# Eighteen weight-chunk casts per mixer on ScalarE instead of VectorE, with the mixer's order laid anew

## The chip, the cores and the metric

One core of one Trainium2 chip runs the whole forward pass. The metric is the device time of one execution in microseconds (us), the median of several. A core has TensorE (PE, matmuls; PEld is its weight loading), VectorE (DVE), ScalarE (ACT), GpSimd (POOL) and SyncE (SP, which here only issues DMAs). Each engine takes its own instruction stream in order. They meet only at semaphores.

## The reference

Two layers over 528 tokens (16 meta tokens and 512 real ones) of width 1024, batch 1. Each layer is a mixer and a convolutional feed-forward network, with fp32 inputs and outputs:

```
xn   = rms_norm(h, norm1_g);  proj = xn @ w_in        # 1024 -> 5288
fq, fk, fv, ff, cq, ckv, krope, sq, sk, sv, gates = split(proj)
out_a = causal_attention(norm(fq), norm(fk), fv, cumsum(log_sigmoid(ff + b)))   # 8 heads x 64
q     = norm(norm(cq) @ w_q_up);  k, v = norm(ckv) @ w_kv_up (+ krope), rope    # 8 heads x 96
out_b = causal_attention(q, k, v)
out_c = sliding_window_attention(norm(sq), norm(sk), sv, sinks, alibi)          # 8 heads, 2 kv heads
h     = h + sum_n(sigmoid(gates_n) * (out_n @ w_branch_n)) @ w_o
u     = rms_norm(h, norm2_g) @ w_up                    # 1024 -> 5632
h     = h + (silu(gate) * val) @ w_down                # gate, val = causal conv of width 3 over u
```

## The kernel before, in words

Weights come from HBM as blocks of 128x128. Eight blocks make a chunk (128x1024 fp32, 512 KB), and 135 chunks make a layer: 61 for the mixer up to the last branch product, then w_o, w_up and w_down. To keep fp32 accuracy each operand is split into a rounded high part and a low part that holds the rest. A block is then three products (high by high, high by low, low by high: L1357, L1360, L1362), each over the two halves of the 528 tokens, so six matmuls.

A chunk passes four stations:

- SP loads it into one of two raw buffers (`load`, L734). It waits until the low part of the chunk two before is made, since that frees the buffer.
- DVE casts it to its high part `wh` (`high_part`, L1670), one of three buffers. It waits for the load and until TensorE has started the chunk two before the cast one.
- POOL subtracts to make the low part `wl` in four pieces (`chunk_low`, L817), after the cast.
- TensorE waits at the first block of a chunk for that (`weights`).

Cast and low part of chunk c stand in their engines' streams where TensorE's stream has block 8(c - 2) of the layer (AHEAD is 2).

The mixer is one list of steps for all engines. `mixer_plan` lays the tiles of the projections in a given ORDER. A tile is 128 output rows: `fq0` is the first pair of query heads of the fox attention, `gF0` a gate tile, `yF0` a product with w_branch, and it takes 8 blocks (y 4, mq 2, mk and mv 1). Every other step gets a block index. The step "newton" of a normed tile stands 4 blocks after its end plus a LATE value, or at BEGIN[job - 2] + 13 if that is later. "norm" is one further on and "high" (ACT's copies of the normed tile into its operands, POOL's low part) two. Twelve attention jobs, each of a pair of heads (4 fox, 4 sliding-window, 4 latent), begin at the indices in BEGIN:

- From BEGIN - 25 the job's scores for the row maximum are computed ("M", L1501) and reduced on DVE (L1962, last the meta rows "MM" at L1940).
- At BEGIN - 4 "NT" transposes the maxima (L1509), and ACT copies them into the query's extra row.
- At BEGIN the scores proper ("STM", "ST", L1540 to L1546) are masked by DVE (L1972, L1985), exponentiated by ACT (L1255, L1258, L1272, L1274) and multiplied with the values ("PV", L1588) two indices later.
- After the second head come four reciprocals on DVE (L1993), the product with them (L1998), and the split of the heads into high and low part.

Each engine's stream is this list sorted by index, with a shift by LAG for chosen pairs of engine and step. So the order is fixed by hand on every engine, and a late instruction holds back all behind it on its engine. START gives the indices, counted from the end of the first tile, of the decay rows of the fox attention ("decay", "decay2"), their way through SP ("extras", L764 and L771) and POOL ("extras2", L918), and the rope rows (L1915 to L1927). ZERO_FIRST and ZERO_AT place POOL's fills of constant rows (L831).

The statistic of an mq tile (L1376) waits for DVE's two products (L1830, L1832), which empty its slot of PSUM.

Of the kernel before, what the change touches and what calls it, by code (L numbers as in the profile page):

```python
# [33 lines left out]
BLK = 8  # L34
CW = BLK * P
RAW, SPLIT = 2, 3
AHEAD = 2
OT_RING = 6
G_RING = 4
PT_RING = 3  # L40
ZERO_FIRST = [0 + n * 2 for n in range(10)]
ZERO_STEP = 2

OFF = np.cumsum([0, 512, 512, 512, 8, 256, 128, 32, 512, 128, 128])
# [36 lines left out]
STAT_LAG = 2  # L81
NORM_LAG = 4
RS_LEAD = 17
BEGIN = [65, 94, 122, 161, 192, 222, 250, 282, 319, 354, 384, 429]
ORDER = 'fk0 gF0 fv0 fq1 fk1 gF1 fk2 fq2 fv1 fk3 fv2 fq3 gF2 sq0 sk gF3 fv3 gF4 sq1 sq2 sv gF6 gF5 yF0 gF7 cq0 cq1 yF1 sq3 yF2 yF3 ckv yF4 yF6 mq0 yF5 mv0 mq1 yF7 gS0 mk0 gS2 mv1 mq2 gS1 gS3 mq3 yS0 mk1 yS1 mq4 gS4 mv2 mq5 yS2 gS5 mk2 gS6 mq6 yS3 gS7 mq7 yS4 yS7 yS5 mk3 gM0 mv3 gM6 gM4 yS6 gM1 gM5 gM7 gM2 gM3'
M_LEAD = 25
M_STEP = 1.8
NT_LEAD = 4
# [1 line left out]
PV_LAG = 2  # L90
ST_END = 13
ZEROS = 10
ZERO_AT = 17
FIRST_STAT = 1
FIRST_LEAD = 16
FIRST_STEP = 0.8
START = [12, 16, 4, 18, 21, 26, 11]
LAG = {('dve', 'layer stat'): 1, ('dve', 'M'): 1, ('dve', 'MM'): 1, ('act', 'O'): -1, ('pool', 'high'): 2, ('act', 'head copy'): 1, ('act', 'tanh'): -1, ('dve', 'rope2'): 1, ('dve', 'decay'): 1, ('dve', 'rope'): 2, ('act', 'inverse'): 4, ('dve', 'heads'): 2, ('act', 'VT'): -1, ('dve', 'join'): 1, ('dve', 'VT'): 1, ('pe', 'MM'): 1, ('dve', 'turn'): 1}

LATE = {'sk': 2, 'cq': 2, 'fv': 1}


def constants():
# [48 lines left out]
    return out  # L154


class Signal:


# [15 lines left out]
class Tile:  # L175


    def __init__(self, kind, m, i):
        self.kind, self.m, self.i = kind, m, i
        self.nk = BLOCKS[kind]  # L180
        self.slot = i % 2
        self.freed = None
        self.joint = None
        self.n = None
        self.raw = None


def mixer_plan():
# [27 lines left out]
    for s in range(2):  # L216
        mine = [t for t in tiles if t.slot == s]
# [4 lines left out]
    events = []  # L222
# [71 lines left out]
    for j, (br, p) in enumerate(JOBS):  # L294
# [17 lines left out]
        for e in range(2):  # L312
            for t in range(5):
                i = b + ST_HEAD * e + t
# [4 lines left out]
        i = b + ST_HEAD + 4 + PV_LAG + 2  # L319
        for q in range(4):  # L320
            put(i + q, 6, "recip", j, q)
        if j >= OT_RING:
            i = max(i, end_of["y", (JOBS[j - OT_RING][0], KD - 1)] - 3)
# [3 lines left out]

    plan = {"tiles": tiles, "order": order}
    for engine in ("pe", "dve", "act", "pool", "sp"):
        mine = [(i + LAG.get((engine, step[0]), 0), rank, n, step) for i, rank, n, step in events]  # L330
        mine = sorted(blocks + mine, key=lambda x: x[0:3])
        plan[engine] = [x[3] for x in mine]


    turn, holder = 0, [None, None, None]
    for s in plan["pe"]:
# [27 lines left out]
        turn = (turn + 1) % 3  # L364
# [21 lines left out]
PLAN = weight_plan(mixer_plan()["order"])  # L386
CHUNKS = DEPTH * len(PLAN) // BLK
# [3 lines left out]
def build(nc, W, H, PRM, CST, POS, OUT, SCR, counts):  # L391
    plan = mixer_plan()
    tiles, order = plan["tiles"], plan["order"]
    LB = len(PLAN)
# [12 lines left out]
    raw = sb("raw", [P, RAW, CW])  # L407
    wh = [sb(f"wh{i}", [P, CW], F32R) for i in range(SPLIT)]
# [44 lines left out]
    sq = sb("sq", [P, 2, T])  # L453
# [48 lines left out]
        return ps[slot][:, CENTRE + j * TH:CENTRE + (j + 1) * TH]  # L502

    signals = []

    def S(name):
        s = Signal(nc, name, counts)
# [7 lines left out]
    s_out = nc.alloc_semaphore("output_stored")  # L515
    s_raw = [nc.alloc_semaphore(f"chunk_loaded{i}") for i in range(RAW)]
    s_hi = nc.alloc_semaphore("chunk_high_part")
    s_lo = nc.alloc_semaphore("chunk_split")
    s_start = nc.alloc_semaphore("chunk_started")
    ready_made = S("small_tiles_ready")  # L520
# [6 lines left out]
    copied = S("tile_copied")  # L527
    squared = S("tile_squared")
# [78 lines left out]
    def frees(t):  # L607
        if t.kind == "ff":
            return rope_copied, ()
        if t.kind in NORMED:  # L610
            if t.kind == "cq" and t.m == 0:
                return copied, (t.i,)
            return (stat_copied if t.kind == "mq" else stat_taken), (t.i,)
        if t.kind in ("fv", "sv"):
            return values_scaled, (t.kind, t.m)
        if t.kind == "mv":
            return values_copied, (t.kind, t.m)
        if t.kind == "g":
            return gate_taken, t.m
        return gate_used, t.m  # L620
# [102 lines left out]
    block = nc.Block()  # L723
    with block as blk:
# [75 lines left out]
        def _(pool):  # L800
# [9 lines left out]
            def chunk_low(c):  # L810
                if c >= CHUNKS:
                    return
                pool.wait_ge(s_hi, c + 1)
                settled()
                for a in range(0, CW, CW // 4):
                    part = slice(a, a + CW // 4)
                    ins = nc.gpsimd.tensor_tensor(wl[c % SPLIT][:, part], raw[:, c % RAW, part],  # L817
                                                  wh[c % SPLIT][:, part].bitcast(F32), ALU.subtract)
                ins.then_inc(s_lo, 1)
                began["last"] = (s_lo, c + 1)  # L820
# [33 lines left out]
            for l in range(DEPTH):  # L854
                n_blocks = 0
                for s in plan["pool"]:
# [9 lines left out]
                    elif s[0] == "zero":  # L866
                        i, n = s[1], s[2]
# [39 lines left out]
                    elif s[0] == "extras2":  # L907
                        j = s[1]
                        br, p = JOBS[j]
                        i = j % 2  # L910
# [3 lines left out]
                        c0, n = (1, T) if br == FOX else (0, TK)  # L914
# [19 lines left out]
                    elif s[0] == "high":  # L934
                        t = s[1]
                        if t.kind in ("fq", "sq"):
                            j = FIRST_JOB[SWA if t.kind == "sq" else FOX] + t.m
                            i = j % 2
# [8 lines left out]
                        elif t.kind == "fk":  # L947
                            j = t.m
                            i = j % 2
# [58 lines left out]
        def _(act):  # L1008
# [39 lines left out]
            for k in range(KD):  # L1048
                if k % 2 == 0:
                    act.wait_ge(s_hin[k // 2], 16)  # L1050
                high_input(0, k)
                nc.scalar.activation(merged[:, k, :], h[:, k, :], ACT.Square).then_inc(
                    residual_squared.sem, residual_squared.tick((-1, "dn", k)))
            for l in range(DEPTH):
                for s in plan["act"]:
                    if s[0] == "layer stat":
                        if s[1] != (l == 0):
                            continue
                        logarithms()
# [2 lines left out]
                    elif s[0] == "done":  # L1062
                        t = s[1]
# [21 lines left out]
                        elif t.kind == "mv":  # L1085
                            act.wait_ge(tile_ready.sem, tile_ready.at(l, t.i))
                            n = value_sets.index(f"{t.kind}{t.m}")
# [4 lines left out]
                    elif s[0] == "stat":  # L1092
                        t = s[1]
                        n = MEAN_OF[t.kind]
# [37 lines left out]
                    elif s[0] == "high":  # L1132
                        t = s[1]
# [10 lines left out]
                        if t.kind in ("fq", "sq", "fk"):  # L1144
                            act.wait_ge(raw_taken.sem, raw_taken.at(l, t.i))
                            dst, high, a = (xk, key_high, 1) if t.kind == "fk" else (xq, query_high, 0)
# [33 lines left out]
                    elif s[0] == "kfill":  # L1180
                        j, e = s[1], s[2]
                        i, kv = j % 2, JOBS[j][1] // 2
# [24 lines left out]
                    elif s[0] in ("VT", "VE"):  # L1207
                        t, second, place = s[1], s[2], s[3]
                        n = value_sets.index(f"{t.kind}{t.m}") + second
# [11 lines left out]
                        for e in range(2):  # L1221
                            c = second if window else e
# [20 lines left out]
                    elif s[0] == "STM":  # L1243
# [8 lines left out]
                        if br == SWA:  # L1252
                            for e in range(2):
                                c = PC_SB + 2 * p + e
# [5 lines left out]
                    elif s[0] == "ST":  # L1260
                        _, j, e, t, place = s
                        br, p = JOBS[j]
                        k0, nk, q0, nq = key_tile(br, t)
                        i = pt_slot(j, e, t)
# [5 lines left out]
                        if br == SWA and t == 0:  # L1270
                            c = PC_SB + 2 * p + e
# [46 lines left out]
                for f in range(FT):  # L1318
                    for side, dst in ((0, cg), (1, cv)):
                        t = 2 * f + side  # L1320
# [341 lines left out]
        def _(dve):  # L1662

            def high_part(c):
                if c >= CHUNKS:
                    return
                dve.wait_ge(s_raw[c % RAW], 16 * (c // RAW + 1))
                if c >= SPLIT:
                    dve.wait_ge(s_start, c - SPLIT + 2)
                nc.vector.tensor_copy(wh[c % SPLIT][:, :], raw[:, c % RAW, :]).then_inc(s_hi, 1)  # L1670

            def advance(l, i):
                n = l * LB + i
                if n % BLK == 0 and n > 0:
                    high_part(n // BLK + AHEAD)
# [91 lines left out]
            for l in range(DEPTH):  # L1767
                n_blocks = 0
# [412 lines left out]
```

## Time and profile before

| what | us |
|---|---|
| median of 3 runs | 1979.04 |
| lowest, highest | 1978.89, 1981.82 |
| profiled execution, first to last instruction (its span, the only time it has) | 1979.4 |
| PE busy | 1914.7 (97%) |
| DVE, POOL, ACT busy | 1159.0 (59%), 1025.5 (52%), 766.2 (39%) |

The two mixers take 31 to 556 us and 1011 to 1540 us of the span. The rest is feed-forward, apart from the first 31 us. The profile's page divides the span into 40 slices of 49.5 us. TensorE is busy for 9 tenths or more in all but three: the first two, and the one at 1039 us, where the second layer has just begun. Engines that are not TensorE are never full. In such a kernel the gaps of TensorE are to be read one by one, with what ended each.

### The profile page before, as it was taken

How to read it: one execution, taken by the hardware profiler on the slowest of the kernel's cores; microseconds unless marked ns; L12 is line 12 of the kernel's file. 1: busy time of each engine (PE TensorE's matmuls, PEld its weight loads, DVE VectorE, ACT ScalarE, POOL GpSimd, SP SyncE). 2: the span in 40 equal slices, each digit the busy share in tenths (PEclk: the TensorE clock that was granted, in tenths of full speed). 3: DMA queues.
4: the chain of work that ended last, by engine and by line, in shares of the span. 5: the costliest groups of instructions: out<-in, count | busy, mean ns of one | idle time of the engine just before them, and what ended most of it. 6: DMA issues, size and time to landing. Idle time of an engine off the chain costs nothing.

```text
span 1979.4 us, 36478 instructions
## 1 busy us (share of the span) xinstructions
PE 1914.7 (97%) x14396; PEld 1817.1 (92%) x14396; DVE 1159.0 (59%) x2121; ACT 766.2 (39%) x1514; POOL 1025.5 (52%) x1306
## 2 busy tenths in 40 slices
PE   7899999999999999999998999999999999999999
PEld 7889998888999999999997899988889999999887
DVE  7665476787465666552256654767874655665411
ACT  5455666655223222220044556666553232222100
POOL 7655454544364444544477455544443645445553
PEclk9999999999999999999999999999999999999999
DMA  4212121211232322332332121112112423323332
GB/s 149 75 44 65 54 65 44 63 45 55 65 129 85 97 86 86 97 93 93 93 109 76 43 65 54 63 46 65 45 53 65 141 86 97 97 86 96 96 97 96
DMA packets 44802, 156.30 MB, mean 79 GB/s; under 512 B 5012, under 2 KB 5268, under 8 KB 44504
## 3 DMA queue, kind: packets, MB, share of 16 engines
q1 hardware_dynamic: 44488, 153.75, 24.7%
q8 instruction: 114, 1.87, 0.4%
q14 instruction: 56, 0.46, 0.1%
q10 hardware_dynamic: 144, 0.22, 0.0%
HBM read 149.63 MB, written 4.26 MB: 78 GB/s over the span
## 4 chain that ended last, share of the span: by engine, by line
PE 77%; DVE 12%; ACT 4%; issue 3%; POOL 2%; DMA 1%; SPq 0%; DVEq 0%; ACTq 0%; POOLq 0%
PE ps L1357 20%; PE ps L1360 19%; PE ps L1362 19%; PE ps L1588 5%; PE ps L1372 2%; PE ps L1368 2%; PE ps L1371 2%; PE ps L1376 2%; DVE osum L1993 1%; DVE rstd L1691 1%; PE ps L1540 1%; PE ps L1501 1%; POOL wl L817 1%; DVE ps L1962 1%; DVE square L1686 1%
## 5 line engine op out<-in xcount | busy, mean ns | idle before, releaser
L817 POOL TENSOR_TENSOR wl<-raw,wh 128x256 fp32r<-128x256 f32 x1076 | 798.7, 773 | 746.5 <-DVE wh L1670 739.9
L1357 PE MATMUL ps<-xh,wh 128*128 128x264 f32 (+1 forms) x2880 | 810.7, 303 | 12.5 <-DVE wl L1750 9.4
L1360 PE MATMUL ps<-xl,wh 128*128 128x264 f32 (+1 forms) x2880 | 764.3, 286 | 0.0
L1362 PE MATMUL ps<-xh,wl 128*128 128x264 f32 (+1 forms) x2880 | 585.4, 285 | 0.0
L1357 PEld LDWEIGHTS ps<-xh,wh 128*128 128x128 f32 x2880 | 546.7, 190 | 31.1 <-issue 18.3
L1360 PEld LDWEIGHTS ps<-xl,wh 128*128 128x128 f32 x2880 | 547.4, 190 | 17.0 <-issue 8.9
L1362 PEld LDWEIGHTS ps<-xh,wl 128*128 128x128 f32 x2880 | 451.2, 190 | 0.0
L1670 DVE CAST wh<-raw 128x1024 fp32r<-128x1024 f32 x270 | 206.6, 765 | 176.0 <-PE ps L1357 89.1
L1588 PE MATMUL ps<-pt,vx 128*128 128x512 f32 (+7 forms) x480 | 157.8, 409 | 3.9 <-ACT pt L1274 2.3
L1985 DVE TENSOR_TENSOR ps<-ps,cst 128x128 f32<-128x128 f32 (+6 forms) x240 | 74.8, 313 | 145.3 <-PE ps L1546 111.0
L1274 ACT ACTIVATE pt<-ps 128x256 f32<-128x256 f32 (+5 forms) x224 | 78.5, 363 | 112.5 <-DVE ps L1985 111.2
L1324 ACT ACTIVATE cv<-ps,prm 128x528 f32<-128x528 f32 (+1 forms) x44 | 34.6, 786 | 209.0 <-DVE ps L2039 209.0
L1357 PE MATMUL ps<-oth,wh 128*128 128x264 f32 (+1 forms) x384 | 111.5, 312 | 2.1 <-ACT ssum L1011 1.7
L2039 DVE TENSOR_TENSOR ps<-ps,rstd 128x528 f32<-128x528 f32 (+1 forms) x88 | 62.1, 706 | 80.5 <-PE ps L1362 80.4
L1360 PE MATMUL ps<-otl,wh 128*128 128x264 f32 (+1 forms) x384 | 100.9, 283 | 0.0
L1993 DVE RECIPROCAL osum<-osum 128x132 f32<-128x132 f32 x96 | 90.0, 958 | 13.2 <-ACT oraw L1011 13.0
L1360 PE MATMUL ps<-al,wh 128*128 128x264 f32 x352 | 93.1, 285 | 0.0
L1357 PE MATMUL ps<-ah,wh 128*128 128x264 f32 x352 | 93.0, 284 | 0.0
L1540 PE MATMUL ps<-xq,xk 97*17 97x16 f32 (+15 forms) x288 | 78.2, 290 | 8.8 <-ACT ptm L1255 4.0
L1501 PE MATMUL ps<-xk,xq 96*128 96x400 f32 (+13 forms) x256 | 71.6, 300 | 9.1 <-DVE nm L1962 3.0
L1588 PEld LDWEIGHTS ps<-pt,vx 128*128 128x128 f32 x480 | 74.6, 191 | 6.2 <-ACT pt L1274 4.1
L1001 POOL TENSOR_TENSOR otl<-oraw,oth 128x528 fp32r<-128x528 f32 x24 | 34.5, 1437 | 87.5 <-ACT oth L1011 86.7
(194 smaller groups left out, 3440.9 us busy)
## 6 DMA issues: line engine op xcount, KB each, us to landing
raw<-weights SPq DMA_DIRECT2D x270, 512.0 KB, 3.5
h<-tokens SPq DMA_DIRECT2D x4, 528.0 KB, 6.9
h<-tokens SPq DMA_DIRECT2D x8, 264.0 KB, 6.0
residual<-h SPq DMA_DIRECT2D x8, 264.0 KB, 5.0
h<-residual SPq DMA_DIRECT2D x8, 264.0 KB, 5.9
out<-h SPq DMA_DIRECT2D x8, 256.0 KB, 4.7
cst<-constants SPq DMA_DIRECT2D x1, 1048.0 KB
extra<-positions SPq DMA_DIRECT2D x18, 4.1 KB
```

The source lines that it names most:

```text
L817: ins = nc.gpsimd.tensor_tensor(wl[c % SPLIT][:, part], raw[:, c % RAW, part], wh[c % SPLIT][:, part].bitcast(F32), ALU.subtract)
L1274: ins = nc.scalar.activation(pt[0:nk, i, 0:nq], bank[0:nk, 0:nq], ACT.Exp)
L1357: a = nc.tensor.matmul(out, a_hi, x_hi[:, sl], start=first, stop=False)
L1360: nc.tensor.matmul(out, a_hi, x_lo[:, sl], start=False, stop=False)
L1362: ins = nc.tensor.matmul(out, a_lo, x_hi[:, sl], start=False, stop=last)
L1501: ins = nc.tensor.matmul(bank[:, col:col + nk], xq[rows, i, e, q], xk[rows, i, e, k0:k0 + nk], start=True, stop=True)
L1540: nc.tensor.matmul(out, xk[rows, i, e, keys], xq[rows, i, e, q], start=True, stop=False)
L1588: ins = nc.tensor.matmul(heads_out[:, c:c + nq], vals, pt[:, i, 0:nq], start=t == 0, stop=t == 4)
L1670: nc.vector.tensor_copy(wh[c % SPLIT][:, :], raw[:, c % RAW, :]).then_inc(s_hi, 1)
L1985: nc.vector.tensor_tensor(sc, sc, cst[0:nk, a:a + n], ALU.add).then_inc(scores_masked.sem, scores_masked.tick((l, j, e, t)))
L1993: nc.vector.reciprocal(osum[:, a:a + T // 4], osum[:, a:a + T // 4]).then_inc(dve_step.sem, dve_step.tick((l, "recip", j, q)))
L2039: nc.vector.tensor_tensor(src[:, skip:T], src[:, skip:T], rstd[:, skip:T], ALU.mult).then_inc(up_scaled.sem, up_scaled.tick((l, t)))
```

## The change

Three things change.

- In each layer the casts of 18 chunks (of the 61 that are made while the mixer runs) move to ACT as `activation(Copy)`. They have a semaphore of their own, `s_hi_act`, on which POOL waits for these chunks. ACT takes such a cast at the block index where DVE had it, with the same two waits.
- The order of tiles, the beginnings of the jobs, START, LATE, LAG, ZERO_FIRST, ZERO_AT and FIRST_STEP get other values, and one single step (`turn mq4` on DVE) is placed one index later (FINE).
- The slot of the tile cq0 is free for TensorE once ACT has squared it, where before it was free once ACT had copied it.

```diff
-ZERO_FIRST = [0 + n * 2 for n in range(10)]
+ZERO_FIRST = [-1, -1, 0, 5, 6, 8, 10, 12, 12, 21]
-BEGIN = [65, 94, 122, 161, 192, 222, 250, 282, 319, 354, 384, 429]
-ORDER = 'fk0 gF0 fv0 fq1 fk1 gF1 fk2 fq2 fv1 fk3 fv2 fq3 gF2 sq0 sk gF3 fv3 gF4 sq1 sq2 sv gF6 gF5 yF0 gF7 cq0 cq1 yF1 sq3 yF2 yF3 ckv yF4 yF6 mq0 yF5 mv0 mq1 yF7 gS0 mk0 gS2 mv1 mq2 gS1 gS3 mq3 yS0 mk1 yS1 mq4 gS4 mv2 mq5 yS2 gS5 mk2 gS6 mq6 yS3 gS7 mq7 yS4 yS7 yS5 mk3 gM0 mv3 gM6 gM4 yS6 gM1 gM5 gM7 gM2 gM3'
+BEGIN = [65, 93, 122, 161, 191, 222, 250, 282, 319, 354, 386, 422]
+ORDER = 'gF0 fk0 fv0 fq1 fk1 gF1 fq2 fv1 fk2 fk3 fv2 fq3 gF2 sq0 sk gF3 fv3 gF4 sq1 sq2 sv gF6 gF5 yF0 cq0 cq1 sq3 yF2 gF7 yF1 yF3 ckv yF4 yF6 mq0 yF5 mv0 mq1 yF7 gS0 mk0 gS2 mv1 mq2 gS1 gS3 mq3 yS0 mk1 yS1 mq4 gS4 mv2 mq5 yS2 gS5 mk2 gS6 mq6 yS3 gS7 yS5 mq7 yS7 yS4 mk3 gM0 mv3 yS6 gM1 gM2 gM6 gM5 gM4 gM3 gM7'
-ZERO_AT = 17
+ZERO_AT = 18
-FIRST_STEP = 0.8
-START = [12, 16, 4, 18, 21, 26, 11]
-LAG = {('dve', 'layer stat'): 1, ('dve', 'M'): 1, ('dve', 'MM'): 1, ('act', 'O'): -1, ('pool', 'high'): 2, ('act', 'head copy'): 1, ('act', 'tanh'): -1, ('dve', 'rope2'): 1, ('dve', 'decay'): 1, ('dve', 'rope'): 2, ('act', 'inverse'): 4, ('dve', 'heads'): 2, ('act', 'VT'): -1, ('dve', 'join'): 1, ('dve', 'VT'): 1, ('pe', 'MM'): 1, ('dve', 'turn'): 1}
-LATE = {'sk': 2, 'cq': 2, 'fv': 1}
+FIRST_STEP = 0.9
+START = [10, 16, 12, 21, 18, 30, 14]
+LAG = {('act', 'O'): -1, ('act', 'head copy'): 2, ('dve', 'M'): 1, ('dve', 'MM'): 1, ('dve', 'heads'): 2,
+       ('dve', 'layer stat'): 1, ('dve', 'rope'): 2, ('dve', 'turn'): 1, ('pe', 'MM'): 1,
+       ('pool', 'head copy'): 2, ('pool', 'high'): 2}
+LATE = {'sk': 2, 'cq': 1, 'fv': 1, 'sv': -1, 'sq': 1, 'fk': 1}
+SCALAR_CASTS = [3, 6, 7, 8, 9, 10, 12, 15, 22, 26, 28, 35, 42, 44, 45, 48, 49, 50]
+FINE = {('dve', 'turn mq4'): 1}
...
+def cast_by_scalar(c):
+    return c % (len(PLAN) // BLK) in SCALAR_CASTS
...
-                pool.wait_ge(s_hi, c + 1)
+                pool.wait_ge(s_hi_act if cast_by_scalar(c) else s_hi, casts[c])
...
+            def high_part(c):
+                if c >= CHUNKS or not cast_by_scalar(c):
+                    return
+                act.wait_ge(s_raw[c % RAW], 16 * (c // RAW + 1))
+                act.wait_ge(s_start, c - SPLIT + 2)
+                copy(wh[c % SPLIT][:, :], raw[:, c % RAW, :]).then_inc(s_hi_act, 1)
...
             def high_part(c):
                 if c >= CHUNKS:
                     return
+                if cast_by_scalar(c):
+                    return
```

In block indices the new order does this. fq2 ends at 72 instead of 80 and fk2 at 88 instead of 72 (fv1 lies between them). cq1 ends at 220 instead of 228 and sq3 at 228 instead of 240, and gF7 moves behind them to 240. The gates of the last branch and three y tiles are shuffled. Jobs 1, 4, 10 and 11 begin 1 earlier, 1 earlier, 2 later and 7 earlier.

## Rows read from the trace of the kernel before

**Rows 1.** Busy time by stage: us, busy us (instructions) of each engine, clock, DMA.
```profile
31.00:556.00 525.00, 502.77 (x3677) 466.74 (x3676) 345.23 (x731) 287.54 (x616) 274.97 (x321) 0.99 0.19 58
556.00:1011.00 455.00, 455.00 (x3725) 454.82 (x3725) 228.91 (x324) 91.59 (x133) 224.88 (x313) 1.00 0.32 99
1011.00:1540.00 529.00, 503.13 (x3726) 466.54 (x3725) 348.61 (x732) 291.59 (x623) 288.11 (x339) 0.99 0.19 58
1540.00:1980.00 440.00, 435.99 (x3157) 411.74 (x3155) 213.92 (x306) 79.80 (x117) 215.86 (x300) 1.00 0.32 99
```
**Rows 2.** Waits of PE, 31 to 556 us: waiter <- awaited: us, times, longest.
```profile
PE ps L1376 <- DVE rawt L1832: 4.1, 4, 1.1
PE ps L1509 <- DVE nm L1940: 2.3, 2, 2.1
PE ps L1540 <- ACT ptm L1255: 2.0, 1, 2.0
```
**Rows 3.** Timeline about 111 us: start, us, instruction [idle before <-releaser].
```profile
106.12 1.76 DVE L1686 TENSOR_TENSOR square<-ssum,square 128x528 f32<-128x528 f32 x1
107.91 0.71 DVE L1691 SCALAR_TENSOR_TENSOR rstd<-square,rstd 128x528 f32<-128x528 f32 x1
108.66 0.77 DVE L1887 SCALAR_TENSOR_TENSOR q<-rawt,gain,rstd 128x528 f32<-128x528 f32 x1
...
111.22 0.33 PE L1509 MATMUL ps<-cst,nm 128*128 128x128 f32 x1 [2.08 <-DVE nm L1940]
```
**Rows 4.** Windows with the clock halved, and one beside them at full clock.
```profile
112.70:116.10 3.40, 3.40 (x18) 3.33 (x17) 0.00 (x0) 2.96 (x10) 3.02 (x3) 0.50 0.00 0
300.40:307.30 6.90, 6.75 (x26) 5.44 (x25) 0.75 (x2) 3.13 (x11) 4.25 (x7) 0.51 0.26 77
307.30:314.00 6.70, 6.70 (x51) 6.37 (x49) 2.59 (x6) 5.58 (x11) 2.81 (x4) 1.00 0.01 2
...
1044.60:1048.00 3.40, 3.40 (x18) 3.32 (x17) 3.34 (x4) 0.48 (x3) 3.21 (x4) 0.51 0.21 40
```
**Rows 5.** Timeline of ACT and PE about 300 us.
```profile
296.81 1.31 ACT L1011 ACTIVATE xq<-q 64x528 fp32r<-64x528 f32 x2 [1.92 <-DVE q L1887]
298.14 1.31 ACT L1011 ACTIVATE yq<-q 64x528 fp32r<-64x528 f32 x2
...
299.95 0.39 PE L1540 MATMUL ps<-xq,xk 97*128 97x256 f32 x1 [1.97 <-ACT ptm L1255]
```
**Rows 6.** The second layer's start: window, timeline, and SP's waits.
```profile
1001.00:1075.00 74.00, 66.25 (x492) 62.62 (x491) 47.98 (x75) 36.12 (x67) 59.90 (x75) 0.98 0.29 94
...
1008.16 2.81 POOL L817 TENSOR_TENSOR wl<-raw,wh 128x256 fp32r<-128x256 f32 x4 [4.96 <-DVE wh L1670]
...
1062.01 1.43 DVE L1670 CAST wh<-raw 128x1024 fp32r<-128x1024 f32 x1 [2.76 <-DMA raw<-weights]
...
SPq L764 <- DVE nd L1868: 11.5, 1, 11.5
```
**Rows 7.** Timeline of DVE and PE where a moved cast precedes a wait.
```profile
322.27 0.74 DVE L1670 CAST wh<-raw 128x1024 fp32r<-128x1024 f32 x1
...
325.93 0.46 PE L1376 MATMUL ps<-sq,cst 96*128 96x264 f32 x1 [0.94 <-DVE rawt L1832]
...
462.57 1.69 DVE L1670 CAST wh<-raw 128x1024 fp32r<-128x1024 f32 x1
...
464.18 0.39 PE L1357 MATMUL ps<-oth,wh 128*128 128x264 f32 x1 [0.86 <-ACT ssum L1011]
```
**Rows 8.** Line L1670, its durations (ns min/median/max), and who waited for it.
```profile
L1670 DVE CAST wh<-raw x270: 618/687/1737, 7.3 to 1959.8; 128x1024 fp32r<-128x1024 f32 x135
...
  POOL wl L817: 739.9, 227
```
**Rows 9.** ACT groups by form: xcount | busy us, mean ns | idle before <-releasers.
```profile
L1011 ACT ACTIVATE oth<-oraw 128x528 fp32r<-128x528 f32 x24 | 15.4, 640 | 61.1 <-DVE oraw L1998 36.6 <-PE ps L1362 24.5
L1129 ACT ACTIVATE gsb<-gsb 128x1056 f32<-128x1056 f32 x12 | 13.0, 1085 | 8.1 <-DVE gsb L1822 8.1
```

More of the change, by code:

```diff
@@ L154, in position_rows, with casts_until @@
     return out
+def cast_by_scalar(c):
+    return c % (len(PLAN) // BLK) in SCALAR_CASTS
+def casts_until():
+    made, counts = [0, 0], []
+    for c in range(CHUNKS):
+        made[cast_by_scalar(c)] += 1
+        counts.append(made[cast_by_scalar(c)])
+    return counts
 class Signal:
@@ L185, in __init__, with step_name @@
         self.raw = None
+def step_name(step):
+    return " ".join(f"{x.kind}{x.m}" if isinstance(x, Tile) else str(x) for x in step if not isinstance(x, dict))
 def mixer_plan():
@@ L329, in mixer_plan @@
     for engine in ("pe", "dve", "act", "pool", "sp"):
-        mine = [(i + LAG.get((engine, step[0]), 0), rank, n, step) for i, rank, n, step in events]
+        mine = [(i + LAG.get((engine, step[0]), 0) + FINE.get((engine, step_name(step)), 0), rank, n, step)
+                for i, rank, n, step in events]
         mine = sorted(blocks + mine, key=lambda x: x[0:3])
@@ L504, in build @@
     signals = []
+    casts = casts_until()
     def S(name):
@@ L517, in build @@
     s_hi = nc.alloc_semaphore("chunk_high_part")
+    s_hi_act = nc.alloc_semaphore("chunk_high_part_by_scalar")
     s_lo = nc.alloc_semaphore("chunk_split")
@@ L611, in frees @@
             if t.kind == "cq" and t.m == 0:
-                return copied, (t.i,)
+                return squared, (t.i,)
             return (stat_copied if t.kind == "mq" else stat_taken), (t.i,)
@@ L1053, in _, with advance @@
                     residual_squared.sem, residual_squared.tick((-1, "dn", k)))
+            def high_part(c):
[4 more added lines that the diff above has]
+                copy(wh[c % SPLIT][:, :], raw[:, c % RAW, :]).then_inc(s_hi_act, 1)
+            def advance(l, i):
+                n = l * LB + i
+                if n % BLK == 0 and n > 0:
+                    high_part(n // BLK + AHEAD)
             for l in range(DEPTH):
+                n_blocks = 0
                 for s in plan["act"]:
-                    if s[0] == "layer stat":
+                    if s[0] == "block":
+                        advance(l, n_blocks)
+                        n_blocks += 1
+                    elif s[0] == "layer stat":
                         if s[1] != (l == 0):
```

## The prediction

> **What bounds the kernel now.** I read the busy times by stage first, then TensorE's waits, then the timeline about each longer wait. The reader sees in [rows 1] that TensorE sets the time everywhere. In the feed-forward from 556 to 1011 us it is busy for all of its 455 us. In the mixers it is busy 502.8 of 525 and 503.1 of 529 us, so 22.2 and 25.9 us are idle, 48.1 together. Matmul durations are modelled and overlap, so a real gap is a little longer than its idle record. DVE has 66% of the mixer (345.2 of 525) and ACT 55% (287.5). Neither is full, and what counts is who is late at one moment. The waits [rows 2] name DVE most: its products for an mq tile (4.1 us), the meta rows' maximum ahead of NT (2.3). ACT's exponentials follow (2.0).
>
> A second loss hides behind the waits. In [rows 4] the granted clock is at half (1.2 instead of 2.4 GHz) for 3.4 us from 112.7 and for 6.9 us from 300.4, and in the second layer from 1044.6; a window at 1102.6 looks like that at 112.7. In 6.9 us at half clock 26 matmuls start, in the 6.7 us behind it 51. So it costs half its length: 1.7 us for a short window, 3.4 for the long one. The windows at 112.7 and 300.4 begin about 1.5 and 0.5 us after TensorE stood 2.08 and 1.97 us [rows 3, 5].
>
> **The change part by part.** The sum is made against the span of the profiled execution, 1979.4 us, which is 0.4 above the median of the runs, so I take the difference for nothing.
>
> *The casts.* 36 go (18 in each layer). A cast on DVE takes 687 ns in the median and up to 1737 [rows 8], so at least 36 x 0.69 = 25 us leave DVE. What TensorE gains is where a moved cast stands in a busy stretch of DVE ahead of what TensorE waits for. Chunk 35's cast (0.74 us at 322.27) is followed without a break by the work up to L1832, for which TensorE waits 0.94: gain 0.74. Chunk 49's cast (1.69 at 462.57) stands ahead of a wait of 0.86 for the slot of a y tile: I count 0.86, though the row names ACT as releaser, since DVE's L1839, which frees the slot, comes only behind the cast [rows 7]. Chunk 44's (0.63 at 414.21) is of the same kind before a wait of 1.46. That makes 2.2 us per layer, 4.5 in all.
>
> *What they cost on ACT.* No row has a Copy of 1024 columns. 528 columns take 640 ns and 1056 take 1085 [rows 9], so 0.84 ns per column and 1.06 us for a cast, 38 us for 36. None of it shows if each falls in a pause of ACT, all 38.1 if each stands ahead of what TensorE waits for. Below nothing it can't go except by what is counted above. Behind a cast queue ACT's exponentials, its row copies for NT and its copies of a finished tile, and TensorE waits for these. The cast's own two waits (the load, TensorE's arrival) now hold ACT's queue and no longer DVE's. I take one in four, 9 x 1.06 = 9.5 us, since ACT is idle 45% of the mixer [rows 1], while its exponentials are among what TensorE waits for longest [rows 2]. POOL waits for the casts 739.9 us in all [rows 8], so 0.4 us more until a low part is ready is hidden by the two chunks of lead.
>
> The Trainium skill, Perfetto Trace Analysis, "Optimizing Scalar/DVE Operations", says that what can run on either engine is faster on DVE where that has a fast mode, and should be offloaded if DVE is saturated. The rows agree on the speed (0.69 against 1.06) and deny the condition (66% busy). By that rule the offload only brings ACT nearer to being the bound, which is the third rival.
>
> *fq2 before fk2, job 1 one index earlier.* Ahead of NT at 111.22, where TensorE stands 2.08 us, DVE works off newton and norm of fq2: 1.76 + 0.71 + 0.77 = 3.24 us [rows 3]. In the new order that tile ends at 72 and its newton stands at 78, fk2's at 93, behind NT at 89. The 3.24 us exceed the wait, so it goes, and with it the half clock: 2.08 + 1.7 = 3.8, and the same in the second layer (I read 2.06 there), 7.5 in all. What is late next is job 2, whose maxima begin at 97, only 4 indices behind the newton of fk2 that feeds them (before, 13 behind 84). Two products, the norm and two copies on ACT are some 3.5 us without queueing. Hidden it costs 0, else about what is gained. I take half: 3.7 back.
>
> *sq3 twelve blocks earlier.* At 296.81 ACT begins four copies of sq3, 2.6 us, and the exponentials of job 6 stand behind them; TensorE waits 1.97 [rows 5]. The newton of sq3 moves from 244 to 235, and the copies from 246 to 237, ahead of the job's begin at 250. The wait goes in both layers (2.04 in the second), and the long half clock of the first [rows 4]: 4.0 + 3.4 = 7.4. In their place two tanh (1.09 each, [rows 9]) and the table load before them move to 241, where they have 9 indices to clear.
>
> *The layer's start.* In the second layer TensorE is idle 7.75 of 74 us, and a half clock costs 1.7 more [rows 4, 6]: 9.4. SP stands 11.5 us at "extras" for the decay rows with weight loads queued behind it, and later DVE stands 2.76 us before a cast whose load is late [rows 6]. Extras moves from 4 to 12 indices behind the first tile, so two more loads go out ahead of it, and that cast (chunk 9) is one of the moved. POOL idles 4.96 us before its first low part there, and two fills of 0.6 to 0.7 us move into that pause. I count half of 9.4, 4.7, and half of that in the first layer, 2.3: 7.0. The extra rows come later for job 0 (extras2 at 21 instead of 18): their cover is that its maxima begin at 49.
>
> *The rest* (the slot of cq0 released later, the LAG entries that go, jobs 4, 10, 11, the last gates) I cost at nothing net. Bounds are 3 us either way, one wait of [rows 7] per layer gained or lost and its neighbours. The largest of these is job 11 begun 7 indices earlier, its maxima now from 397, six behind the newton of mk3 at 391. The instructions in number and the loads stay the same, and the 895 us outside the mixers are untouched [rows 1].
>
> Sum: 4.5 + 7.5 + 7.4 + 7.0 = 26.4 gained, 9.5 + 3.7 = 13.2 lost, 13.2 net. 1979.4 - 13.2 = 1966.2; I say 1966.
>
> **The rivals.**
>
> *One wait for another.* The removed waits come back at the next late step, fk2 at 97 and mk3 at 391, with their half clocks. For it: DVE is behind in long stretches, so a step moved away lands in another. Against: the four large waits have their own causes, which move by 8 indices and more. Only the casts' 4.5 us remain, less some on ACT: 1975 to 1980, say 1978.
>
> *The shared port.* A cast takes 0.62 us at best and 1.69 at 462.57, 1.74 at most [rows 7, 8], and the long ones lie beside POOL's work. If DVE and POOL hold each other up, moving 36 casts frees both, and DVE's other work shortens too. Then the 9.5 us of ACT are met by as much on DVE, and no new wait of 3.7 appears: 1979.4 - 26.4 - 3 = 1950. Against it: the long casts are few, the median being 0.69. The Trainium skill, SBUF — State Buffer, "SBUF: two separate sides", has that as its rule: DVE's fast copies and GpSimd take one port pair under an exclusive lock, and ScalarE has its own; the long casts agree.
>
> *ACT becomes the bound (the other side).* A cast of 1.06 us stands before ACT's exponentials, for which TensorE has only a three-deep ring and two indices of lead (about 2 us). If all 36 show, the time is 1979.4 - 26.4 + 38.1 = 1991; with 3.7 for fk2 it decides from 21 casts shown on, (26.4 - 3.7) / 1.06. For it: a single queue of ACT 2.6 us long made TensorE wait 1.97 [rows 5]. Against: ACT goes from 55% to 58%, and that queue was longer than a cast.
>
> *The change doesn't do what it says:* the casts on ACT bring nothing, and only the new order works: 1979.4 - 7.5 - 7.4 + 3.7 = 1968. It can't be told from the forecast by time.
>
> **How the numbers follow.** Forecast 0.50 (own range 1958 to 1974), new order alone 0.10, shared port 0.12, one wait for another 0.13, ACT the bound 0.15. What this kernel's measurement can tell from no change is about 0.2%, 4 us. Slower by more takes nearly all of the last case (0.14) and a little of the wait for a wait (0.02): 0.16. Within 0.2% are the rest of these and the forecast's edge: 0.12. Faster: 0.72. The range that leaves out 2 in 10, one at each end, is 1951 to 1984.
>
> **What would show it.** Right: no wait at L1509 near 110 us and at L1540 near 300, and the half clocks after them gone; idle TensorE in the two mixers down from 48 to about 35 us; ACT casts of 1.06 us; DVE busy down by 25 to 30 us; fewer late loads at the second layer's start. Wrong: waits of TensorE for ACT's pt, ptm or row copies grow by more than 10 us; a new wait at L1501 for the keys of job 2 or 11; half clocks at new places; ACT casts far from 1.06 us. A time over 1975 would mean that stalls move rather than go.

## The result, and the profile after

| | median us | runs | ratio to before (95% interval) |
|---|---|---|---|
| before, same chip | 1980.43 | 4 (1978.89 to 1982.94) | |
| changed | 1967.14 | 4 (1963.26 to 1972.35) | 0.9933 (0.9917 to 0.9949) |
| changed, measured again | 1964.89 | 4 (1963.94 to 1967.17) | 0.9921 (0.9908 to 0.9934) |

The ratio of the last row is to 11 runs of before on its own chip (median 1980.00). Both intervals leave out 1. The forecast was 1966. The profiled execution is the slowest of the four, 1972.35 us with a span of 1970.6, against 1981.82 and 1979.4 before. So the spans differ by 8.8 us, the medians by 13.3.

Busy times by stage in the changed kernel, columns as in [rows 1]:

```profile
31.00:550.00 519.00, 500.64 (x3663) 464.40 (x3663) 324.06 (x712) 302.41 (x632) 271.66 (x318) 0.99 0.19 58
550.00:1005.00 455.00, 455.00 (x3726) 454.84 (x3725) 229.74 (x325) 90.99 (x133) 223.71 (x312) 1.00 0.31 97
1005.00:1531.00 526.00, 503.87 (x3743) 467.78 (x3742) 329.80 (x714) 309.50 (x642) 286.23 (x341) 0.99 0.20 61
1531.00:1971.00 440.00, 436.17 (x3158) 411.81 (x3157) 213.18 (x306) 79.82 (x117) 215.89 (x300) 1.00 0.32 98
```

TensorE is idle 18.4 and 22.1 us in the two mixers, 40.5 together where it was 48.1. Both feed-forwards have their old 455 and 440 us. DVE's share of the first mixer fell from 66% to 62%, ACT's rose from 55% to 58%.

What TensorE waits for in the first mixer (compare [rows 2]):

```profile
PE ps L1584 <- ACT pt L1318: 3.1, 4, 1.4
PE ps L1420 <- DVE rawt L1878: 3.1, 4, 1.1
PE ps L1584 <- ACT ptm L1302: 2.2, 2, 1.9
PE ps L1545 <- ACT pt L1318: 2.2, 2, 1.2
...
PE ps L1545 <- ACT xk L1037: 1.1, 1, 1.1
```

The wait before NT has gone and that for DVE's rawt is down from 4.1 to 3.1. At the head of the list stand ACT's exponentials. The casts on ACT, from the instructions grouped by line and form:

```profile
L1037 ACT ACTIVATE wh<-raw 128x1024 fp32r<-128x1024 f32 x36 | 38.0, 1054 | 12.6 <-PE ps L1401 6.6 <-DMA raw<-weights 5.5
```

and those on DVE, from the page:

```profile
L1716 DVE CAST wh<-raw 128x1024 fp32r<-128x1024 f32 x234 | 170.6, 729 | 167.8 <-PE ps L1401 90.5
```

A cast on ACT is 1.054 us (1.06 was estimated). DVE's casts fell from 206.6 to 170.6 us. Not all of that is the move: with the new order alone they take 198.5 us (735 ns in the mean instead of 765), so the 36 moved casts account for 27.9 us, 0.78 each, and those that stayed take 729 ns.

The clock is at half in other places. Windows in the changed kernel, the second at full clock:

```profile
81.70:88.50 6.80, 6.80 (x22) 4.94 (x21) 0.60 (x2) 1.83 (x8) 4.65 (x6) 0.50 0.28 80
88.50:95.30 6.80, 6.80 (x52) 6.41 (x51) 2.75 (x10) 3.34 (x7) 0.75 (x2) 1.00 0.00 0
126.00:129.40 3.40, 3.40 (x13) 3.09 (x14) 0.00 (x0) 0.00 (x0) 2.42 (x2) 0.50 0.46 154
```

The half clocks of [rows 4] at 112.7, 300.4, 1044.6 and 1102.6 are gone. In their place are one of 6.8 us from 81.6 and short ones from 126.0, 1068.1 and 1109.0, each behind new or longer waits. In these two executions the mixers have the same time at half clock, so the 8.8 us between the spans are not the clock's.

Over all runs it is a part. Every run lists its span and mean granted clock. Span x clock is what the run would have taken at full clock, to about 1 us since the clock has three digits, and span x (1 - clock) is what the half clock cost it. The last column is how long TensorE is idle in the two mixers of the profiled execution:

| kernel | casts on ACT per layer | ratio to before | span x clock, median | span x (1 - clock), median | TensorE idle |
|---|---|---|---|---|---|
| before (19 runs beside the second to fifth row) | 0 | 1 | 1971.2 | 9.9 | 48.1 |
| order alone | 0 | 0.9975 (0.9965 to 0.9985) | 1967.4 | 5.9 | 46.4 |
| casts alone | 18 | 1.0014 (1.0005 to 1.0023) | 1970.8 | 11.9 | 52.1 |
| changed, 54 casts | 54 | 1.0028 (1.0017 to 1.0040) | 1978.3 | 6.0 | 55.9 |
| changed without chunk 10 | 17 | 0.9915 (0.9902 to 0.9929) | 1957.4 | 4.9 | 37.6 |
| changed | 18 | 0.9933 (0.9917 to 0.9949) | 1960.3 | 5.9 | 40.5 |
| changed, three casts | 3 | 0.9942 (0.9928 to 0.9955) | 1963.3 | 3.9 | 42.4 |
| changed, fk2 back | 18 | 0.9981 (0.9972 to 0.9991) | 1963.4 | 13.8 | 45.2 |
| changed, sq3 back | 18 | 0.9978 (0.9969 to 0.9986) | 1967.0 | 9.9 | 44.8 |
| changed, start back | 18 | 0.9952 (0.9939 to 0.9964) | 1960.2 | 11.8 | 41.2 |

So about 11 us of the change are time at full clock, and the rest is less loss at half clock. The split is rough: before's own four sets of runs have 1971.0 to 1972.1 at full clock and 5.9 to 9.9 lost. The changed kernel's own runs show what the clock does: spans of 1961.5, 1963.0, 1967.7 and 1970.6 at 1.000, 0.998, 0.996 and 0.995.

### The profile page after: what moved, and what is told of

The parts are those of the page before. It is cut to its first block, busy times and chain, and to the rows that moved or that the text cites. A ratio compares the mean times of both kernels' runs of the same rounds, so it can differ in the third digit from the quotient of the medians.

```text
span 1970.6 us, 36481 instructions
## 1 busy us (share of the span) xinstructions
PE 1912.9 (97%) x14396; PEld 1815.4 (92%) x14396; DVE 1119.8 (57%) x2085; ACT 799.5 (41%) x1550; POOL 1020.5 (52%) x1306
## 3 DMA queue, kind: packets, MB, share of 16 engines
q8 instruction: 114, 1.87, 0.4%
## 4 chain that ended last, share of the span: by engine, by line
PE 81%; DVE 9%; ACT 6%; issue 3%; DMA 0%; SPq 0%; ACTq 0%; DVEq 0%
PE ps L1401 21%; PE ps L1404 21%; PE ps L1406 21%; PE ps L1632 5%; PE ps L1420 2%; PE ps L1416 2%; PE ps L1412 2%; PE ps L1415 2%; PE ps L1545 1%; PE ps L1584 1%; DVE rstd L1737 1%; DVE osum L2039 1%; ACT square L1054 1%; ACT rstd L1055 1%; PE ps L1590 1%
## 5 line engine op out<-in xcount | busy, mean ns | idle before, releaser
L1716 DVE CAST wh<-raw 128x1024 fp32r<-128x1024 f32 x234 | 170.6, 729 | 167.8 <-PE ps L1401 90.5
L1406 PE MATMUL ps<-oth,wl 128*128 128x264 f32 (+1 forms) x384 | 77.3, 283 | 0.0
```

The lines of the kernel that those rows point to most:

```text
L1406: ins = nc.tensor.matmul(out, a_lo, x_hi[:, sl], start=False, stop=last)
```

## The experiments

**The order alone and the casts alone**

```diff
-SCALAR_CASTS = [3, 6, 7, 8, 9, 10, 12, 15, 22, 26, 28, 35, 42, 44, 45, 48, 49, 50]
+SCALAR_CASTS = []
```

> The changed kernel with no cast on ScalarE: all 61 of a mixer stay on VectorE, the new order stays. Theory A (the order carries the gain, the casts are worth about as much on one engine as they cost on the other): within 3 us of the changed kernel, 1964 to 1970. Theory B (the casts carry it; the order was laid for them): the waits behind VectorE's casts come back, 4.5 us by the sum of the prediction or more, 1972 to 1982. At block 67, where ScalarE's cast of chunk 10 (1.06 us) stands straight ahead of the exponential that TensorE waits 1.87 us for, the wait should shrink by about 1 us by either.

The casts alone are the changed kernel's code with BEGIN, ORDER, START, LATE, LAG, ZERO_FIRST, ZERO_AT and FIRST_STEP of before, and no FINE.

> The kernel before with only the 18 casts of each mixer moved to ScalarE, old order, old lags. Theory A: about the time before less 4.5 us for the casts plus up to 9.5 us on ScalarE, so 1976 to 1986. Theory B: 1970 to 1976. The four large waits (NT at block 90, the exponential at block 252, in each layer) should still be there, each at 1.3 to 2.1 us, with half clocks behind some.

Measured: order alone 1975.65 us, ratio 0.9975; casts alone 1984.50, 1.0014; before, of the same rounds, 1981.70. Theory A fails for the order: it carries 0.25%, about 5 us, and the other 8 to 9 us come when the casts move under it. In the old order the same casts cost 3 us, which theory A allowed and theory B excluded. So neither holds for both halves. They are worth -5 and +3 us alone and -13 to -15 together. The profile of the casts alone shows where the 3 us arise, about the wait of [rows 3]:

```profile
107.56 1.06 ACT L1035 ACTIVATE wh<-raw 128x1024 fp32r<-128x1024 f32 x1
108.53 0.63 ACT L1052 ACTIVATE square<-ssum 128x528 f32<-128x528 f32 x1
...
110.54 0.86 DVE L1730 TENSOR_TENSOR square<-ssum,square 128x528 f32<-128x528 f32 x1 [0.77 <-ACT square L1054]
111.43 1.12 DVE L1735 SCALAR_TENSOR_TENSOR rstd<-square,rstd 128x528 f32<-128x528 f32 x1
112.59 1.51 DVE L1931 SCALAR_TENSOR_TENSOR q<-rawt,gain,rstd 128x528 f32<-128x528 f32 x1
114.02 1.80 DVE L2042 TENSOR_TENSOR oraw<-oraw,osum 128x528 f32<-128x528 f32 x1
...
117.00 0.47 PE L1551 MATMUL ps<-cst,nm 128*128 128x128 f32 x1 [4.35 <-DVE nm L1984]
```

ACT's cast of chunk 12 stands ahead of the three activations that start fq2's newton. DVE, relieved of that cast, now waits 0.77 us for them. The four instructions that follow take 5.29 us together, where before they took 3.94: the square 0.86 instead of 1.76, but the next three 1.12, 1.51 and 1.80 instead of 0.71, 0.77 and 0.70 ([rows 3], and for the last):

```profile
109.34 0.70 DVE L1998 TENSOR_TENSOR oraw<-oraw,osum 128x528 f32<-128x528 f32 x1
```

TensorE waits 4.35 us before NT instead of 2.08, in both layers. These two waits alone are 4.6 us more, and its idle time in the mixers is 4.0 us more. The new order has no such chain ahead of NT.

In the new order the gain of three casts can be read behind the chunks that the prediction named. The order alone, then the changed kernel, about block 380 of the first layer:

```profile
457.45 1.32 DVE L1716 CAST wh<-raw 128x1024 fp32r<-128x1024 f32 x1
458.80 0.71 DVE L1876 TENSOR_TENSOR rawt<-ps,gq 32x528 f32<-32x528 f32 x1
459.53 0.70 DVE L1878 TENSOR_TENSOR rawt<-ps,gq 96x528 f32<-96x528 f32 x1
...
460.38 0.46 PE L1420 MATMUL ps<-sq,cst 96*128 96x264 f32 x1 [2.30 <-DVE rawt L1878]
```

```profile
459.84 0.14 DVE L2008 DVE_READ_ACCUMULATOR2_ANT nmx<- 128x1 f32 x1
460.01 0.71 DVE L1876 TENSOR_TENSOR rawt<-ps,gq 32x528 f32<-32x528 f32 x1
460.74 0.70 DVE L1878 TENSOR_TENSOR rawt<-ps,gq 96x528 f32<-96x528 f32 x1
...
461.59 0.46 PE L1420 MATMUL ps<-sq,cst 96*128 96x264 f32 x1 [0.69 <-DVE rawt L1878]
```

Chunk 49's cast stands straight ahead of the two products of mq7 that TensorE waits for. Without it the wait is 0.69 instead of 2.30. But it is not the wait that the prediction counted, and most of the gain repairs what the new order did: before, mq7 ended four blocks earlier, its products ran ahead of that cast, and TensorE waited 1.08 us for them.

**Three casts instead of eighteen**

```diff
+SCALAR_CASTS = [35, 44, 49]
```

> The new order with only the casts of chunks 35, 44 and 49 on ScalarE, the three that the prediction named. In the profile of the order alone TensorE waits 0.89, 1.44 and 2.30 us at the places behind them (blocks 268, 339, 380), in the changed kernel 0.29, 0.92 and 0.69: 2.7 us less per layer. If each wait depends on its own cast, these three waits are those of the changed kernel, all others those of the order alone (at the layer's start 2.27 and 3.57 us at block 44, 1.24 at 51), and the time is 5.4 us below the order alone: about 1970. If the gain lies in what VectorE is relieved of over the whole mixer, the time stays at 1974 to 1976.

Measured: 1969.23 us, 0.9942. Behind chunks 35 and 44 TensorE waits 0.29 and 0.89 us, as in the changed kernel, behind chunk 49 1.12 instead of 2.30. The waits at the layer's start stay (2.98 and 3.58 us at block 44). So three casts of eighteen bring about 6 of the 8 to 9 us, and of the 5.9 us less that TensorE is idle they bring 4.0. The other fifteen together bring some 2 us, and here the intervals of three casts and of the changed kernel overlap. They take from the waits at the layer's start (2.98 us at block 44 of the first layer becomes 1.30) and give to the one at block 67 (0.79 becomes 1.87, for ACT).

**Fifty-four casts**

```diff
+SCALAR_CASTS = list(range(3, 57))
```

> The changed kernel with all casts of chunks 3 to 56 on ScalarE, 54 in each mixer instead of 18, 72 more in all. If ScalarE's queue is what a cast costs (1.06 us each when all show) the time rises by up to 76 us; by the prediction's one in four, 72 x 0.265 = 19 us less what VectorE is relieved of, say 1974 to 1984. If ScalarE has room and VectorE is the late engine, it does not rise: 1960 to 1968. TensorE's waits for the exponentials pt and ptm tell: 19 us in all in the changed kernel's profile.

Measured: 1986.52 us, 1.0028. That is 18.8 us over the changed kernel by the ratios (0.0095 x 1980) and 0.26 us for each of the 72 casts, a quarter of 1.06. The expected quarter was the cost on ACT alone, while the measured one has what DVE is relieved of already in it, so that the two agree is chance. The expected 1974 to 1984 was low by 2.5. TensorE's waits of 0.3 to 0.5 us at blocks 124, 148 and 258 become 1.4 and more. Two forces act at once, seen in the wait lists of this kernel:

```profile
PE ps L1420 <- DVE rawt L1878: 12.3, 12, 1.9
...
PE ps L1584 <- ACT ptm L1302: 7.3, 4, 2.5
PE ps L1545 <- ACT pt L1318: 5.9, 8, 1.0
PE ps L1584 <- ACT pt L1318: 5.5, 8, 1.2
```

The waits for ptm grew from 4.6 to 7.3 us, and all those for pt and ptm together from 17.7 to 25.3. Those for rawt grew from 6.6 to 12.3, though DVE has fewer casts: its product waits for ACT's square (L1113). At 384.07 us, where TensorE's wait is 1.91, DVE stands 2.10 us for a square that has a cast, a table load and two tanh ahead of it on ACT.

**One cast back, and two more places**

```diff
-SCALAR_CASTS = [3, 6, 7, 8, 9, 10, 12, ...]
+SCALAR_CASTS = [3, 6, 7, 8, 9, 12, ...]
```

> The changed kernel with the cast of chunk 10 of each layer back on VectorE. It stands straight ahead of job 0's first exponential on ScalarE, where TensorE waits 1.87 and 1.97 us at block 67. If the cast is what makes that wait, it shrinks by 1.06 us per layer, and the long half clock that begins behind it (6.8 us at half, 3.4 us lost) goes: 2 to 5.5 us less than the changed kernel, 1961 to 1965. If the four copies of a key tile ahead of it are enough to hold TensorE, the wait stays above 1 us and the time does not move.

The changed kernel has on ACT, ahead of the first exponential of job 0:

```profile
78.67 1.31 ACT L1037 ACTIVATE yk<-q 64x528 fp32r<-64x528 f32 x2
80.00 1.06 ACT L1037 ACTIVATE wh<-raw 128x1024 fp32r<-128x1024 f32 x1
81.08 0.19 ACT L1302 ACTIVATE ptm<-ps 17x32 f32<-17x32 f32 x1
...
81.32 0.39 PE L1584 MATMUL ps<-xq,xk 97*128 97x272 f32 x1 [1.87 <-ACT ptm L1302]
```

and without chunk 10's cast:

```profile
80.26 0.39 PE L1584 MATMUL ps<-xq,xk 97*128 97x272 f32 x1 [0.80 <-ACT ptm L1302]
```

The wait shrinks by 1.07 us, the length of the cast, and in the second layer from 1.97 to 0.87; no half clock follows. The time was 1964.09 us (0.9915). To compare it with the changed kernel beside it, both were run again:

> The changed kernel itself, on the chip and in the rounds of the next two, so that they can be compared with it. By its first runs (1963.3 to 1972.4) the time should lie at 0.991 to 0.995 of before, and its runs should differ by their mean granted clock: about 2 us for each 0.001 of it.

> The changed kernel with chunk 10's cast on VectorE, again. If the 1.06 us of that cast ahead of job 0's first exponential is what the wait at block 67 consists of, it is faster than the changed kernel of the same rounds by 2 to 5 us. If the first comparison was the clock's doing, the two are within 2 us.

Changed 1964.89 us, 0.9921 (0.9908 to 0.9934), without chunk 10 1964.12, 0.9914 (0.9902 to 0.9927). The full-clock times were 1959.3 and 1957.5. The medians are 0.8 us apart, within the 2 us that the expectation named as the clock's doing. The waits are shorter by 2.1 to 2.2 us in both pairs of profiles, but the times overlap: 1 to 3 us is what can be said. Nor does the half clock hang on this cast. In the second profile of the changed kernel TensorE waits 1.85 us at block 67 of the first layer, as in the first (1.87), and no half clock follows, where the first had 6.8 us of it.

The next step added two FINE entries for fk2 and two for the key copies of job 6:

```diff
+FINE = {..., ('dve', 'newton fk2'): -1, ('dve', 'norm fk2 0'): -1, ('act', 'high fk2'): -1,
+        ('act', 'kfill 6 0'): -3, ('act', 'kfill 6 1'): -3}
```

> The changed kernel, chunk 10's cast on VectorE, and two more small moves. The newton and norm of fk2 on VectorE and its high part on ScalarE stand one index earlier, against the waits of 1.1 and 0.95 us at blocks 97 and 98. The six key copies of job 6 on ScalarE stand three indices earlier, against the wait of 1.43 us at block 225, ahead of which they and a statistic's three activations hold ScalarE. If each wait is made by what stands ahead of it in the queue, 2 to 5 us less than without chunk 10 alone: 1959 to 1962. If the next late step takes over, within 1 us of it, 1963 to 1965.

Measured: 1971.85 us, 0.9948 (0.9936 to 0.9960), 7 us slower than without chunk 10 alone. In that profile:

```profile
115.44 0.19 ACT L1302 ACTIVATE ptm<-ps 17x32 f32<-17x32 f32 x1 [2.49 <-DVE ps L2018]
...
115.68 0.40 PE L1584 MATMUL ps<-xq,xk 97*128 97x272 f32 x1 [1.60 <-ACT ptm L1302]
...
264.18 0.61 ACT L1037 ACTIVATE rawt<-ps 128x528 f32<-128x528 f32 x1
...
265.32 0.71 DVE L1829 TENSOR_TENSOR sq<-sq 128x528 f32<-128x528 f32 x1 [6.88 <-ACT sq L1119]
...
266.18 0.46 PE L1420 MATMUL ps<-sq,cst 128*128 128x264 f32 x1 [2.96 <-DVE sq L1829]
```

The waits of 1.11 and 0.94 us at blocks 97 and 98 became one of 1.60 at block 95, and the one of 1.43 at 225 became 2.96 at 223: the key copies now hold ACT's copy and square of cq1, and DVE's step on that square, for which TensorE waits, comes late with them. Then the other way about:

```diff
+FINE = {..., ('dve', 'newton fk2'): -1, ('dve', 'norm fk2 0'): -1}
-LATE = {..., 'cq': 1, ...}
+LATE = {..., 'cq': 2, ...}
```

> Without chunk 10's cast on ScalarE, the newton and norm of fk2 one index earlier on VectorE only (ScalarE's copies stay behind job 1's exponentials, since moving them ahead made TensorE wait 1.6 us for pt at block 95), and the statistic of cq1 one index later on all engines, behind job 5's exponential at block 225. If both waits (1.11 and 1.43 us per layer) are queueing alone, 2 to 5 us below the kernel without chunk 10; if fk2's copies don't start earlier and the statistic only comes late for the norm, within 1.5 us of it.

Measured: 1965.17 us, 0.9924 (0.9912 to 0.9936), no gain. The wait at block 95 stays at 1.56, so it was DVE's newton ahead of job 1's masks that made it (ACT idles 2.49 us for the mask L2018 above), not ACT's copies, as I had written. The wait at 225 is now 1.51 us, for the exponential of another step. No version tried is clearly faster than the changed kernel without chunk 10.

**Three parts of the order undone, one at a time**

```diff
-gF1 fq2 fv1 fk2 fk3     BEGIN[1] = 93     # fk2 back
+gF1 fk2 fq2 fv1 fk3     BEGIN[1] = 94
...
-yF0 cq0 cq1 sq3 yF2 gF7 yF1 yF3          # sq3 back
+yF0 gF7 cq0 cq1 yF1 sq3 yF2 yF3
...
-gF0 fk0    START, ZERO_FIRST, ZERO_AT and FIRST_STEP of the change   # start back
+fk0 gF0    those of before
```

> The changed kernel with one place of the order undone: fk2, fq2, fv1 again in that order and job 1 again at 94. By the prediction's step the move was worth the wait before NT (2.08 us) and its half clock per layer, less new waits for fk2's keys: the profile of the change has these (1.11 and 0.94 us at blocks 97 and 98). If the step is right, the wait at block 90 returns, the two at 97 and 98 go, and the time is 2 to 10 us above the changed kernel. With casts on ScalarE the wait at 90 may be larger than 2.08: in the kernel with the casts alone it was 4.35. If the two places are worth the same, within 2 us.

Measured 1979.05 us (a run of 5901.68 us aside), 0.9981: 9.5 us over the changed kernel by the ratios, 12 by the medians.

```profile
117.21 0.48 PE L1553 MATMUL ps<-cst,nm 128*128 128x128 f32 x1 [4.35 <-DVE nm L1986]
```

The wait before NT returns, and at 4.35 us, as with the casts alone. By the table's medians only 3 us are time at full clock, and 8 are lost at half clock. In that profile the clock is at half for 6.8 us from 115.6 and for 6.8 from 1102.1, at both of these waits.

> The changed kernel with gF7, cq0, cq1, yF1, sq3, yF2 again in the order of before. If the early sq3 is what took the wait of 1.97 us at block 252 away, that wait returns in both layers and the one of 1.43 at block 225 goes or shrinks: 1 to 5 us above the changed kernel. If the wait only moved from 252 to 225, within 2 us of it.

Measured 1978.67 us, 0.9978: 9 us over by the ratios. By the table's medians 7 are at full clock and 4 lost at half clock. TensorE is only 4.3 us longer idle, and where the rest of the 7 lies no profile shows. The expected 5 at most was too low. The wait at block 252 returns with 1.58 us (1.63 in the second layer), and others of 0.59, 0.90 and 0.70 appear at 222, 224 and 244 where the changed kernel has 1.43 at 225.

> The changed kernel with the layer's start undone: fk0 before gF0, and START, ZERO_FIRST, ZERO_AT and FIRST_STEP as before. The prediction gave the start 7 us of gain. If that is right, the time is 4 to 10 us above the changed kernel, with the wait for late weights at block 40 (1.2 us) back. If the start gave nothing, within 2 us; the profile of the change still has 2.64 us at block 44 and 1.97 at block 67 there.

Measured 1973.80 us, 0.9952: 3.8 us over by the ratio, with intervals that overlap. The time at full clock is the same (1960.2 against 1960.3) and the idle time nearly so (41.2 against 40.5), so what the start gives is less loss at half clock, if anything. The waits at block 40 were 0 and 2.50 us and that at 67 2.82 and 2.85, where the changed kernel has 1.30 and 2.64 at block 44 and 1.87 and 1.97 at 67.

The three undoings add to 22 us, more than the whole change gives. Like order and casts they can't be added up.

## Why the prediction was right, and where only its sum was

**The total** was right (13.2 net, measured 13.3 and, again, 15), but by luck: the errors of two terms cancel. The prediction gave the order 21.9 us less 3.7 and the casts -4.5 + 9.5 = 5 of loss. Measured alone, the order gives 5 and the casts lose 3; under the new order the casts gain 8 to 9. The order alone, which the rival of that name priced at 1968, stood at 1975.65. That price left out the 7.0 us of the layer's start; with them the prediction's own terms give 1961. The failed assumption is that the parts add up. Each cast's worth depends on what the order puts behind it on DVE and on ACT.

**The casts' gain**, 4.5 us by chunks 35, 44 and 49. These three bring 6 under the new order, but one of them not by the prediction's mechanism. The profile of the casts alone tests the terms in the old order. The wait behind chunk 35 falls from 0.94 to 0.29 us (0.74 was counted) and the one behind chunk 44 from 1.46 to 0.91 (0.63 was counted), while the wait of 0.86 behind chunk 49 stays:

```profile
468.80 0.39 PE L1399 MATMUL ps<-oth,wh 128*128 128x264 f32 x1 [0.85 <-ACT ssum L1035]
```

So the row that names ACT was right, and the reading against it was wrong. In the trace of before ACT's copy of ssum ends at 464.12 us and TensorE goes on at 464.18, the moment at which DVE's L1839 only begins. What chunk 49 is worth in the new order, 1.6 us in the first layer, is another wait, that for mq7's products.

**The casts' cost on ACT**, one in four of 1.06. The size of a cast was right to 1%, and 0.26 us for each further cast is what 72 more showed. For the 18 casts no run separates the cost on ACT from the gain on DVE; the one that stands straight ahead of an exponential, chunk 10, costs 1.07 and 1.10. In the old order the largest cost came by a way that the prediction did not have: TensorE waits before NT for DVE, and DVE had waited for ACT's activations and then taken longer over its own instructions.

**fq2 before fk2**, 7.5 gained and 3.7 back. The wait before NT went in both layers, as said, and fk2's keys came late as said, at block 97 (1.11 us, for ACT's xk) and 98 (0.94). The half clocks, however, did not go: they moved to 126.0 and 1109.0, behind the two new waits. The mis-sized term is what comes back: in both layers the two new waits (2.05 us together) are as long as the one removed (2.08 and 2.06), and half was counted. Measured against the kernel before, the place gains nothing. Undoing it costs 9.5 because, with casts on ACT, the wait that it brings back is 4.35.

**sq3 twelve blocks earlier**, 7.4. The waits of 1.97 and 2.04 us and the long half clock at 300.4 are gone, and 1.43 at block 225 is new in both layers; the prediction named no successor. Net that is 1.2 us of waits and, in the two profiles, 3.4 of half clock: 4.6 instead of 7.4. Undoing it cost more, 9 us. ACT holds it there with key copies and a statistic's activations:

```profile
270.12 0.64 ACT L1037 ACTIVATE yk<-skl 64x528 fp32r<-64x528 f32 x1
270.79 0.65 ACT L1054 ACTIVATE square<-ssum 128x528 f32<-128x528 f32 x1
271.46 0.64 ACT L1055 ACTIVATE rstd<-square 128x528 f32<-128x528 f32 x1
272.14 0.64 ACT L1056 ACTIVATE square<-rstd 128x528 f32<-128x528 f32 x1
...
273.11 0.33 PE L1584 MATMUL ps<-xq,xk 97*128 97x146 f32 x1 [1.43 <-ACT pt L1318]
```

**The layer's start**, 7.0. The causes were right and did go: SP stands 3.6 us at extras instead of 11.5, and no cast on DVE waits for a late load. But TensorE is idle as long as before:

```profile
995.00:1069.00 74.00, 66.34 (x508) 63.12 (x507) 43.72 (x70) 41.87 (x73) 60.17 (x78) 0.99 0.31 97
```

(the window of busy times) and, from the waits of SP's queue:

```profile
SPq L790 <- DVE nd L1914: 3.6, 1, 3.6
```

It is 7.66 us idle here against 7.75 [rows 6], and 5.10 against 5.36 from 31 to 85 us in the first layer, at other places: block 44 for fv0's values, which stand on DVE behind the rope rows and a newton and norm, and 67. The term of 7.0 is mis-sized: nothing of it is found in waits, and the 3.8 us measured by undoing it are half of it, are the clock's, and are not clear of noise.

**The signs** that the prediction named came out on both sides. Right were the end of the two large waits, ACT's casts of 1.054 us and the late loads. TensorE's idle time fell from 48.1 to 40.5 us and not to about 35. DVE's busy time fell by 39 us in all, of which 25 lie between the order alone and the changed kernel. Of the signs of being wrong two came, a new wait for the keys of job 2 (1.11 us) and half clocks at new places. TensorE's waits for pt and ptm grew by 2.0 us, far less than the 10 named.

**The rivals.** "One wait for another" was true in kind at three of four places, but with the smaller price. "ACT the bound" is 36 casts further on: with 54 per layer the kernel is slower than before. "The shared port": the long casts became fewer (765 to 729 ns in the mean, 735 with the order alone), and DVE's L1691 fell from 927 to 878 ns (895 with the order alone), but POOL's low parts did not change (773 and 772 ns), so it is not where the time came from. The Trainium skill, SBUF — State Buffer, "SBUF: two separate sides", would let one side block the other. DVE's part of it shows in the 1.51 and 1.80 us of the casts-alone profile, which begin while POOL works at 3.12 us of key tiles (from 112.14 us); on POOL's side no run here shows a gain. The Trainium skill, Perfetto Trace Analysis, "Optimizing Scalar/DVE Operations", names a saturated DVE as the case in which offloading may make sense. Here the gain did not hang on that: at 66% busy three chosen casts were worth 6 us, and 36 more per layer lost 19.

The slot of cq0, the dropped LAG entries and the last gates were not tried by themselves.

## What to carry to other kernels

Choose what to move between two engines by what stands directly behind it on either queue, one instruction at a time, not by the engines' shares: three casts of eighteen gave most of what the casts gained, one cost a microsecond per layer. Believe the row that names who ended a wait, unless the times of both engines speak against it. Test such a move together with the order it is meant for, since alone it can have the other sign. After removing a wait look for the next late step and for the half clock behind it, which can cost more than the wait (3.4 us behind one of 1.97).

## What was not expected of the hardware

The granted clock makes a large part of this kernel's scatter. In the changed kernel it went from 0.995 to 1.000 from run to run with 9 us of span between, and kernels whose TensorE waits 4.35 us at one place had medians of 0.993 and 0.994, the others here 0.994 to 0.998. With fk2 back 3 us were lost at full clock and 8 by the clock. But the tie to waits is loose: the kernel with 54 casts has the most idle time (55.9 us) and a median clock of 0.997, and one and the same wait of the changed kernel was followed by 6.8 us of half clock in one execution and by none in another. What decides that stays open.
